# PEER sublayer of a hybrid encoder layer: 224 instead of 256 dense tokens, gates multiplied in place on chip, sums with the features on the partitions

## The reference, cut to what matters

```
hid = jnp.einsum('thkd,td->thk', u[e], xt)
act = jax.nn.gelu(hid.astype(f32), approximate=False)
out = jnp.einsum('thk,thkd->td', (g * act).astype(v.dtype), v[e])
x = layer_norm(ALPHA * x + ffn, ln2_g[l], ln2_b[l])
```

## Time and profile before

| | |
|---|---|
| median of three runs | 1580.42 us |
| span of the profiled execution | 1607.5 us |
| PE busy / weight loads busy | 1534.6 us (95%) / 1090.8 us (68%) |
| DVE busy | 1115.6 us (69%) |
| ACT busy | 274.6 us (17%) |
| POOL busy | 618.2 us (38%) |
| data moved | 532.39 MB, 331 GB/s on average |
| fronts A and B | 0 to 652.5 us |
| blocks 0 to 50 of `hidden` | 652.5 to 832.35 us |
| blocks 51 to 127 with `spread` | 832.35 to 1160.7 us |
| `combine` | 1160.7 to 1600.2 us |

### The profile page before, as it was taken

One profiled execution on the slowest core, in us unless ns is written; L12 is line 12 of the kernel. 1 busy time (PEld: TensorE's weight loads), 2 busy tenths in 40 slices (PEclk: granted clock), 3 DMA queues, 4 the chain that ended last, 5 costly groups with the idle time before them and its releaser, 6 DMA issues.

```text
span 1607.5 us, 17999 instructions
## 1 busy us (share of the span) xinstructions
PE 1534.6 (95%) x6542; PEld 1090.8 (68%) x6542; DVE 1115.6 (69%) x2434; ACT 274.6 (17%) x543; POOL 618.2 (38%) x516
## 2 busy tenths in 40 slices
PE   7999998689999879999999999999999999999998
PEld 7798687555558446788889999888844444444443
DVE  1413899877769948999949888899564545555472
ACT  2601114711010111111123333333100000000000
POOL 0000646537655522212215555567443342424210
PEclk9999998879999879999999999999999999999999
DMA  8586988758999866788879999999999999999972
GB/s 324 178 285 220 357 313 295 268 197 316 412 393 383 314 260 209 280 302 296 297 265 362 414 414 417 414 412 406 409 372 384 382 390 386 391 389 384 405 260 90
DMA packets 142856, 532.39 MB, mean 331 GB/s; under 512 B 15024, under 2 KB 30128, under 8 KB 130480
## 3 DMA queue, kind: packets, MB, share of 16 engines
q0 software_dynamic: 73728, 268.47, 44.3%
q1 hardware_dynamic: 68176, 250.19, 41.4%
q10 hardware_dynamic: 864, 12.58, 1.8%
HBM read 503.92 MB, written 27.26 MB: 330 GB/s over the span
## 4 chain that ended last, share of the span: by engine, by line
PE 74%; DVE 11%; DMA 7%; issue 4%; ACT 2%; SPq 0%; POOL 0%; another core or an unknown queue 0%; DVEq 0%
PE bank L899 27%; PE bank L875 22%; PE bank L763 7%; PE bank L855 6%; DMA arena<-u_d,arena 5%; DVE arena L1210 4%; PE bank L893 2%; PE bank L775 2%; PE bank L777 2%; DMA arena<-u_cols_d 1%; PE bank L605 1%; DVE arena L1229 1%; DMA arena<-w_items_d 1%; DVE arena L1437 1%; PE bank L579 1%
## 5 line engine op out<-in xcount | busy, mean ns | idle before, releaser
L1655 POOL DMA_INDIRECT arena<-u_d,arena x256 | 343.1, 1340 | 419.1 <-DVE arena L1592 167.1
L1655 POOL DMA_INDIRECT arena<-v_d,arena x256 | 275.0, 1074 | 496.2 <-DVE arena L1229 411.2
L875 PE MATMUL bank<-arena 128*128 128x256 f32 x2048 | 456.0, 381 | 5.5 <-DMA arena<-u_cols_d 5.5
L899 PE MATMUL bank<-arena 128*128 128x512 f32 x1024 | 439.6, 592 | 0.0
L875 PEld LDWEIGHTS bank<-arena 128*128 128x128 f32 x2048 | 386.0, 191 | 56.2 <-issue 4.0
L899 PEld LDWEIGHTS bank<-arena 128*128 128x128 f32 x1024 | 194.6, 190 | 244.5 <-issue 242.3
L1210 DVE CUSTOM_DVE_ANT_0 arena<-arena 128x1024 f32<-128x1024 f32 x256 | 303.0, 1220 | 31.3 <-DMA arena<-u_d,arena 30.3
L1229 DVE SCALAR_TENSOR_TENSOR arena<-arena 128x1024 f32<-128x1024 f32 x254 | 320.9, 1285 | 0.3
L1557 DVE TENSOR_TENSOR arena<-arena 128x192 f32<-128x192 f32 x128 | 45.2, 353 | 199.4 <-DMA arena<-act_d 158.6
L855 PE MATMUL bank<-arena 128*128 128x128 f32 (+1 forms) x512 | 122.9, 397 | 15.1 <-issue 13.7
L855 PEld LDWEIGHTS bank<-arena 128*128 128x128 f32 x512 | 80.2, 197 | 54.0 <-issue 23.2
(11 more groups left out here) (203 smaller groups left out, 1100.0 us busy)
## 6 DMA issues: line engine op xcount, KB each, us to landing
arena<-w_items_d SPq DMA_DIRECT2D x66, 1024.0 KB, 9.4
arena<-u_cols_d SPq DMA_DIRECT2D x128, 512.0 KB
arena<-v_cols_d SPq DMA_DIRECT2D x128, 512.0 KB, 12.9
act_d<-arena SPq DMA_DIRECT2D x12, 1024.0 KB
gates_d<-arena ACTq DMA_DIRECT2D x6, 2048.0 KB
arena<-gates_d SPq DMA_DIRECT2D x16, 768.0 KB, 13.1
arena<-act_d SPq DMA_DIRECT2D x12, 1024.0 KB, 15.8
arena<-u_d,arena POOLq DMA_INDIRECT x256
```

Source lines behind the costliest of these rows:

```text
L875: last = mm(bank[:, 4 + c % 2, 0:ND], u_buf[:, c % UBUFS, k, :], B.act_in[:, k, B.n - ND:B.n], start=k == 0, stop=k == KC - 1)
L899: return mm(bank[:, 2 * n + half, :], act_slot(i)[:, n * P:(n + 1) * P], v_buf[i % VBUFS][:, half * 512:(half + 1) * 512], start=i == 0, s ...
L1655: pool.indirect_dma_start(rows[:, r % SLOTS, :], None, table, bass.IndirectOffsetOnAxis(eidx[:, t, k:k + 1], 0)).then_inc(landed[r % SLOTS ...
```

## The change

The dense tokens become 224: the last `XT` = 32 tokens of tile 3 leave them. For these 32 tokens the 128 picks are laid over the 128 partitions (4 groups of 32 partitions with 32 picks each), so that 32 gathers of u and 32 of v, appended to the 512, do them (`extra_row`); a product with a folded identity adds the four groups (`fold_extra`).

Activations are no longer spilled and gates no longer stored. One buffer of 128 blocks x 224 tokens (`w_low`, 45 blocks, and `w_high`, 83 blocks) stays on chip. When a group of four tokens has been spread after block c, VectorE multiplies its gates from PSUM into all the blocks that are there (`take_gates`), and ScalarE copies the gates of the blocks that are still to come into their places (`copy_gates`), where `weigh` multiplies the activation in as soon as it exists. The buffers for this come from 8 instead of 12 row buffers, from x1 (saved to DRAM and read back) and from what the fronts no longer need. VectorE only compares for the one-hots; the multiplication by the gate is done by ScalarE, one token at a time (`scale_hot`). `combine` takes the v block as weights (8 pieces of 128 features) and the 224 tokens as columns; its sums have the features on the partitions and are turned back at the end (`copy_sums`, `turn_sums`).

```diff
-SLOTS = 12
+SLOTS = 8
...
+XT = 32
+XR = NE // KG
...
+ALL_ROWS = 4 * NE + 2 * XR
-ND = len(DENSE) * P
+ND = len(DENSE) * P - XT
...
-EXP_AT = 49
-TURN_AT = 51
-SPREAD_AT, SPREAD_END = 52, 120
+EXP_AT = 53
+TURN_AT = 55
+SPREAD_AT, SPREAD_END = 56, 122
...
-HOT_ROWS = 126
-MID_ROWS = 374
+HOT_ROWS = 124
+MID_ROWS = 368
...
-                    load_act(b)
...
-                    pe.wait_ge(g_out, q - 1)
+                    pe.wait_ge(g_used, q - 1)
...
-                return mm(bank[:, 2 * n + half, :], act_slot(i)[:, n * P:(n + 1) * P],
-                          v_buf[i % VBUFS][:, half * 512:(half + 1) * 512],
+                return mm(bank[:, m // 2, m % 2 * 256 + tokens.start:m % 2 * 256 + tokens.stop],
+                          v_buf[i % VBUFS][:, m * P:(m + 1) * P], w_block(i)[:, tokens],
...
+                order = [(n, b) for n in range(len(DENSE)) for b in range(KC // 2)]
+                for k, (n, b) in enumerate(order):
+                    last_sums(n, b)
+                    if k:
+                        turn_sums(*order[k - 1])
+                    if k == 2:
+                        fold_extra()
+                turn_sums(*order[-1])
...
-                fn(act_ring[c % RINGED_ACT], bank[:, 4 + c % 2, 0:ND], ACT.Gelu).then_inc(act_done, 1)
+                    last = fn(act_new[k % len(act_new)][:, 0:n], src[:, 0:n], ACT.Gelu)
+                if n < ND:
+                    last = fn(w_block(c)[:, n:ND], src[:, n:ND], ACT.Gelu)
+                last.then_inc(act_done, 1)
...
-                fn(stage[g % 2][:, :, k * QUAD:(k + 1) * QUAD].rearrange("p e t -> p t e"),
-                   bank[:, 6 + q % 2, :].rearrange("p (t e) -> p t e", t=QUAD), ACT.Copy).then_inc(g_out, 1)
+                fn(w_high[:, c + 1 - LOW:, q * QUAD:(q + 1) * QUAD],
+                   bank[:, 6 + q % 2, :].rearrange("p (t e) -> p e t", t=QUAD)[:, c + 1:, :], ACT.Copy).then_inc(g_out, 1)
...
+            def scale_hot(q):
...
+                act.wait_ge(hot_raw, q + 1)
...
+                for j in range(QUAD):
+                    one = hot[:, q % 2, QUAD + j, :]
+                    last = fn(one, one, ACT.Copy, scale=gT[d][:, t + j:t + j + 1])
...
+            def take_gates(q, c):
+                dve.wait_ge(act_done, c + 1)
+                dve.wait_ge(g_out, q + 1)
...
+                low = w_low[:, :, ts].rearrange("p e t -> p t e")
+                high = w_high[:, 0:top, ts].rearrange("p e t -> p t e")
+                v.tensor_tensor(low, low, g[:, :, 0:LOW], ALU.mult)
+                v.tensor_tensor(high, high, g[:, :, LOW:c + 1], ALU.mult).then_inc(g_used, 1)
...
+            for c in range(SPREAD_AT, EXPERTS + 1):
+                for q in range(quads_by(c), quads_by(c + 1)):
+                    one_hot(q)
+                if ahead(c - 1):
+                    weigh(c - 1)
+                for q in range(quads_by(c - 2), quads_by(c - 1)):
+                    take_gates(q, c - 1)
+                rows_until(first + HOT_ROWS * (c + 1 - SPREAD_AT) // (EXPERTS + 1 - SPREAD_AT))
+            rows_until(ALL_ROWS)
...
+            extra_sum()
```

More of the change, by code:

```diff
@@ L100, with ahead, weighed_by @@
 ROPE, SOFT_ARG, V_ZERO, KQ = 1, 2, 3, 4
-def rows_at(i):
-    return min(4 * NE, MID_ROWS + int(3.2 * min(i, EXPERTS - FIRST)) + int(1.1 * max(0, i - EXPERTS + FIRST)))
-NORM1_W = min(i for i in range(EXPERTS) if rows_at(i) == 4 * NE)
 def quads_by(c):
     return min(QUADS, max(0, (c - SPREAD_AT + 1) * QUADS // (SPREAD_END - SPREAD_AT)))
+def ahead(b):
+    return QUAD * quads_by(b - 1)
+def weighed_by(b):
+    return sum(ahead(k) > 0 for k in range(b + 1))
 def at_mix(m):
@@ L224, in build @@
         gsum = view(197.75, PH)
[L227 to L233, removed]
+        w_low, w_high = view(48, LOW, ND), view(116, EXPERTS - LOW, ND)
+        hot = view(96, 2, 2 * QUAD, NK)
+        x1_back, ln2_gb = view(48, len(DENSE), D), view(56, 2, D)
+        x_rep, x_acc = view(64, D), view(68, D)
+        yT = view(72, KC, ND)
         top = view(176, PH, 2, TOPK)
@@ L903, in combine, with w_done @@
+            def w_done(i):
+                if weighed_by(i):
+                    pe.wait_ge(w_ready, weighed_by(i))
             def combine(i):
-                pe.wait_ge(w_ready, i + 1)
+                w_done(i)
                 pe.wait_ge(v_in[i % VBUFS], 16 * (i // VBUFS + 1))
-                for n in range(len(DENSE)):
-                    for half in range(2):
-                        last = sums(i, n, half)
+                for m in range(KC):
+                    last = sums(i, m, slice(0, ND))
@@ L923, in _, with last_sums @@
-            for c in range(FIRST):
+            def last_sums(n, b):
+                if n:
+                    pe.wait_ge(yT_out, b + 1)
+                for m in (2 * b, 2 * b + 1):
+                    for i in range(EXPERTS - LAST, EXPERTS):
+                        if n == m == 0:
+                            w_done(i)
+                            pe.wait_ge(v_in[i % VBUFS], 16 * (i // VBUFS + 1))
+                        last = sums(i, m, slice(n * P, n * P + WIDTH[n]))
+                last.then_inc(o_done, 1)
@@ new lines, in turn_sums, with fold_extra @@
+            def turn_sums(n, b):
+                pe.wait_ge(yT_out, 4 * n + b + 1)
+                for m in (2 * b, 2 * b + 1):
+                    last = turn(bank[0:WIDTH[n], 4 + 2 * n + m // 4, m % 4 * P:(m % 4 + 1) * P],
+                                yT[:, m, n * P:n * P + WIDTH[n]], ident[:, :])
+                last.then_inc(y_turned, 1)
+            def fold_extra():
+                pe.wait_ge(x_acc_ready, 1)
+                for half in range(2):
+                    last = mm(bank[X0:P, 6 + half, :], fold[:, :], x_acc[:, half * 512:(half + 1) * 512], start=True, stop=True)
+                last.then_inc(x_folded, 1)
@@ L1156, in _, with copy_sums @@
             hid_gelu(1)
-            for n in range(1, T):
-                root(n)
+            root(0)
+            root(1)
+            act.wait_ge(hid_ready, 4)
+            fn(x_hid[:, :], x_hid[:, :], ACT.Gelu).then_inc(gelu_done, 1)
+            fn(pos_f[:, 0:1], pos_f[:, 0:1], ACT.Sqrt)
+            def copy_sums(n, b):
+                act.wait_ge(o_done, EXPERTS - LAST + 4 * n + b + 1)
+                part = slice(n * P, n * P + WIDTH[n])
+                fn(yT[:, 2 * b:2 * b + 2, part], bank[:, b, :].rearrange("p (m t) -> p m t", m=2)[:, :, part],
+                   ACT.Copy).then_inc(yT_out, 1)
+            for b in range(4):
+                copy_sums(0, b)
+            copy_sums(1, 0)
+            copy_sums(1, 1)
+            root(2)
+            copy_sums(1, 2)
+            copy_sums(1, 3)
+            root(3)
         @block.vector
```

410 lines of the change are left out of this document (208 added, 202 removed).

## The result

| | before | after |
|---|---|---|
| time, median of 4 runs of each (us) | 1579.68 (1573.35 to 1584.03) | **1551.70** (1547.29 to 1554.53) |
| ratio | | 0.9835, 95% interval 0.9801 to 0.9869 |
| profiled execution: time, span (us) | 1573.84, 1571.9 (a second profile) | 1551.54, 1549.7 |
| dense half: start to end of the kernel (us) | 619.1 to 1571.9: 952.8 | 630.7 to 1549.7: 919.0 |
| combining starts (us) | 1125.0 | 1073.8 |

The change gains 28 us (1.65%); the forecast was a gain of 75, within a range that holds the measured time. The profile of the kernel before on which the prediction rests had a long front part: its dense half starts at 652.5 us. The second profile of the same kernel starts it at 619.1, and both give the dense half the same length, 952.8 and 955.0 us. So comparisons of the dense half hold with either, and for the front I use the second.

The account below looks back on a forecast made before the run. TensorE bounds the dense half, with DMA queues and VectorE close behind. TensorE's -110, VectorE's +9 while spreading and +26 waiting for the last rows make -75 us: 1580.4 to 1505 us, range 1470 to 1565.

Parts of the forecast that it names:

- TensorE's terms: Dense half on TensorE: 224-column records at 189.2 ns, shorter `hidden`, spreading, sums and stalls, longer tail; together 110 us less.
- Rival D: Dense half: 224 columns take as long as 256 because the weight load sets the pace; about 1577 us; chance 0.04.
- The price of the stride: `take_gates` on VectorE while spreading: elements 224 apart cost ScalarE's 0.93 ns more per element, taken once, 19 us.
- The steps: Blocks 56 to 121, while spreading: VectorE needs 259 us against TensorE's 250, so combining starts 9 us later.
- Rival B: VectorE's strided `take_gates` costs both ways, 38 us instead of 19, giving 1524, or more, about 1546; chance 0.22.
- The queues while combining: Before the fold: 320 transfers take 405 us against TensorE's 382, so TensorE stands still for 26 us.
- The two fronts are costed at nothing: Before the dense half: eight instead of twelve row buffers and 1 MB of x1 saved cost 0 us.
- rival C: Eight row buffers starve the gathers, slower than before: 1797 us at unchanged latency, deciding from 16.8 us; chance 0.07.

## Why the prediction was right and wrong

**TensorE's terms held.** A record of 224 columns was put at 189.2 ns and takes 189.3. The sums were put at 375.4 us and take 375.5. Combining was to start 450.5 us after the dense half and starts 443. The whole, -110 us or 1470, is borne out by the two kernels that lift the queues: 1480 without the extra rows and 1476 with half v blocks. Their dense halves both last 843.7 us, 109 less than the 952.8 before; their fronts are 14 and 8 us longer. Rival D (224 columns as slow as 256) is out.

**The price of the stride held, its effect did not.** The nearest row gave 0.93 ns more per element; VectorE pays (499 - 355) / 180 = 0.80. The operand in PSUM has no part in it as far as the rows show, since beside each other its elements cost nothing (549 against 558 ns for 384); no run takes the stride alone away, and the products of 176 to 188 elements without it scatter from 330 to 398 ns. From the start of one piece to the next it is 0.40 us (942.59 to 942.99 us), where 0.43 was forecast, 0.26 for no charge and 0.6 for both ways. The "cachelines" note of the Trainium skill (SBUF — State Buffer) has a penalty for each access that goes to a new line. The trace agrees that VectorE pays one too, once and not for the read and the write, which would have given 1524.

The steps did not hold up TensorE either, as I had it with 9 us: it waited 0.6 us for them. VectorE came out just short of a full stage, 198.1 of 200 us. The experiments at this place show that its load there has a price nevertheless. A multiplication put back on it cost 33.6 us, with combining 33 us later and the two waits as long as before. 16 rows taken from it cost 26, with combining on time and the waits 23 us longer. Rival B (both ways) did not come.

**The step that failed is "The queues while combining".** It put TensorE's wait at 26 us and the trace shows 71. By its own terms:

| | forecast | measured |
|---|---|---|
| transfers after combining begins | 200 rows + 120 v | 212 gathers and 125 v issued, others, and what was in flight, counted from 1067 us, 7 before it |
| in units of 0.524 MB | 320 | 349 |
| rate | 414 GB/s | 406 to 1450 us, then 367 to the last landing |
| time of the transfers | 405 us | 457 us, to the last landing at 1524 |
| from the last landing to the fold | 2.5 us | 3.8 us |
| TensorE until the fold | 382 us | 383 us |

Of the 457 us, 7 lie ahead of the first sum, so 450 count: 45 more than forecast. 29 more units at 1.27 us make 37, the lower rates 15, and the 7 go off. With 1.3 and -1 from the last lines, 26 becomes 71. So the mechanism was right and its size was not: the number of transfers was put too low, and the rate at the end too high. The miscount has three sources. About 12 rows were counted as used that VectorE did not get to. Some v blocks were counted as loaded ahead and were not: 120 were to be left, and 125 were still issued. And x1 coming back, the norm's constants, the extra tile's input and the output are 3.7 MB, 7 units, that the count left out. The rest of the 29 was in flight at 1067 us.

**The end of that stretch has another limiter.** From 1450 us on only gathers are left, and the rate falls (27.1 MB until 1524 us, 367 GB/s; the 352 of the table has 3 idle us in it). The waits of GpSimd in that stretch:

```profile
POOL arena L1755 <- issue: 14.0, 46, 0.3
POOL arena L1755 <- DVE x_hid L1244: 1.2, 2, 0.6
POOL arena L1755 <- DVE arena L1255: 0.6, 1, 0.6
```

Until its last issue, which ends at 1519 us, GpSimd is busy for 53.7 us and between its own issues for 14.0, and it waits 1.8 us for buffers. One gather takes it 1.10 + 0.30 = 1.40 us, more than the 1.27 us that the queues need. This reading rests on the trace alone: no kernel here issues gathers faster, and the queues' share is 0.97 until 1524 us, so which of the two sets this stretch is not shown.

**"The two fronts are costed at nothing" was wrong by about 12 us.** The start of the dense half shows it (630.7 against 619.1), and so do eight buffers in the kernel before (635.0, and 13.4 us in the median, part of which is lost in its dense half). While combining, rival C fails: gathers took 13.8 us there in the median, under the 16.8 from which it was to decide (some on the chain took up to 18.7), and six buffers brought almost the same rate. But the prediction named its place too narrowly. The buffers matter where few other transfers keep the queues full.

**The balance**, in spans: the forecast had the dense half at 955 - 75 = 880 us, and it takes 919. Combining starts 443 us after the dense half and not 450.5; the fold comes 454 us after that and not 407.5; and what stands behind the fold takes 22 us, as forecast. So 7 come off and 46.5 go on, 45 of them the longer wait. The fronts add 12. From profile to profile this is 22 us less than before, from median to median 28. The 6 us between them lie within the spread of single runs of the kernel before, 1573 to 1587.

Not tried: more row buffers in the changed kernel, for which there is no space, a smaller added group than 32 tokens, and ScalarE's Gelu of the extra tile behind the copies of the sums, which would take the first wait off TensorE but not the rows off the queues.

## What to carry to other kernels

When the leading engine is relieved, count every transfer from the stage in question to the end of the kernel, the small ones and those that an earlier stage leaves over included, and hold their sum against the queues; here they had been hidden by a few per cent and became the next bound. Time on an engine for which nobody waits is not free if that engine paces the transfers: queue time unused in one stage has to be made up in a later one that has none to spare. A buffer count is to be judged in every stage that waits for those buffers: here fewer buffers cost time in the fronts and ahead of the spreading, and next to nothing in the fullest stage.

## What the hardware showed beyond expectation

- With the queues full, the latency of a gather follows the number in flight and says nothing of the rate: 12.1 us with eight buffers and 9.0 with six, at 409 and 405 GB/s.
- Full queues (a DMA share of 1.02 or 1.03) moved 403 to 409 GB/s while combining in the changed kernels that compute everything with eight buffers, and 406 to 415 while spreading in the kernel before, the lowest with its buffers cut to eight (stretches of 200 us and more). At a share of 1.00 it was 388 in the kernel before, where a third of the packets was under 2 KB, and 386 with half v blocks. Gathers alone made 367 at 0.97, with GpSimd's 1.40 us per issue as the likely reason.
- Elements 896 bytes apart take VectorE 499 ns for 180, with one operand in PSUM, against 355 ns for a product with neither, 0.80 ns more per element. An operand in PSUM with its elements side by side cost nothing: 549 against 558 ns for 384, and 284 against 292 for 128.
- While TensorE stood still for 31 and 40 us its granted clock fell to 0.50, and the first records after the second wait took 1057 ns each instead of 592. The fold and the sums right behind it lasted some 2 us longer by that.
- Two profiles of the same kernel differed by 33 us in the time at which the dense half starts and by 2 in all that follows. A sum made against one profile should be checked for the stage in which its excess lies.
